# Two down projections computed by seven block products in place of eight

## What is computed

```
# first block
up = conv(h @ w_up) ; val, gate = split(up)
x = x + g2 * ((silu(gate) * val) @ w_down)       # (1024, 2816) @ (2816, 1024)
# second block
a, g = split(h @ ffn_up) ; a = dwconv3x3(a) + b
x = x + gate * ((gelu(a) * g) @ ffn_down)         # the same sizes
```

## Time and profile before

| what | value |
|---|---|
| median of three runs | 2507.37 us |
| the profiled execution | 2507.51 us |
| its span, first to last instruction | 2505.7 us |
| first down projection, first matmul to first of the short units | 904.93 to 1138.49 us |
| short units behind it | 1138.49 to 1183.55 us |
| second down projection to the end of its last unit | 2249.02 to 2487.53 us |
| rows behind it, to the end | 2487.53 to 2505.7 us |

### The profile page before, as it was taken

One profiled execution on the slowest core, in us unless ns is written; L12 is line 12 of the kernel. 1 busy time (PEld: TensorE's weight loads), 2 busy tenths in 40 slices (PEclk: granted clock), 3 DMA queues, 4 the chain that ended last, 5 costly groups with the idle time before them and its releaser, 6 DMA issues. The chain is left out here.

```text
span 2505.7 us, 38163 instructions
## 1 busy us (share of the span) xinstructions
PE 2390.1 (95%) x16353; PEld 1291.5 (52%) x16353; DVE 1634.7 (65%) x2158; ACT 1019.3 (41%) x1219; POOL 561.4 (22%) x296
## 2 busy tenths in 40 slices
PE   7989889999999999999999999988989999999997
PEld 3447664444444444444767776774434444444443
DVE  6788847565545554555477878786878877773343
ACT  5117417345454531323354545442344444441221
POOL 0010000057777711000000000000036766630000
PEclk9999999999999999999999999999999999999998
DMA  9117674121212144443200000003112121225342
GB/s 338 34 53 237 195 229 160 62 73 52 67 51 68 51 148 122 110 109 127 64 26 18 26 26 23 21 26 126 51 51 67 51 68 51 68 64 176 94 114 90
DMA packets 307687, 224.62 MB, mean 90 GB/s; under 512 B 11424, under 2 KB 298302, under 8 KB 306367
## 3 DMA queue, kind: packets, MB, share of 16 engines
q1 hardware_dynamic: 306646, 221.86, 29.3%
q10 hardware_dynamic: 873, 0.32, 0.1%
HBM read 199.61 MB, written 22.03 MB: 88 GB/s over the span
## 5 line engine op out<-in xcount | busy, mean ns | idle before, releaser
L200 PE MATMUL ps<-hT,arena 128*128 128x512 bf16 (+1 forms) x2592 | 552.4, 374 | 15.8 <-DVE arena L2185 5.9
L2118 PE MATMUL ps<-hT,arena 128*128 128x512 bf16 x2280 | 498.9, 379 | 0.3 <-DVE ps L2269 0.3
L1923 PE MATMUL ps<-arena 128*128 128x512 bf16 x2106 | 459.0, 380 | 2.5 <-DVE arena L1907 2.5
L200 PEld LDWEIGHTS ps<-hT,arena 128*128 128x128 bf16 x2592 | 252.7, 98 | 313.3 <-issue 20.3
L2118 PEld LDWEIGHTS ps<-hT,arena 128*128 128x128 bf16 x2280 | 223.0, 98 | 269.8 <-issue 1.3
L1923 PEld LDWEIGHTS ps<-arena 128*128 128x128 bf16 x2106 | 206.3, 98 | 251.8 <-DVE arena L1907 3.8
L2194 POOL TENSOR_TENSOR arena<-arena 128x2048 f32<-128x2048 f32 x2 | 12.6, 6282 | 1138.7 <-DVE arena L696 1138.7
L2407 DVE SCALAR_TENSOR_TENSOR xT<-ps,vec,xT 128x945 f32<-128x945 f32 (+2 forms) x176 | 215.1, 1222 | 31.9 <-ACT xT L2390 26.4
L1907 DVE TENSOR_TENSOR arena<-hT,arena 128x2816 bf16<-128x2816 f32 x30 | 92.8, 3093 | 181.8 <-ACT arena L1902 181.6
L2118 PE MATMUL ps<-xT,arena 128*128 128x512 bf16 x912 | 203.0, 379 | 0.0
L2185 POOL TENSOR_TENSOR arena<-arena 128x2048 bf16<-128x2048 f32 x38 | 156.4, 4115 | 100.6 <-ACT arena L2177 100.6
(11 more groups left out here) (454 smaller groups left out, 3291.8 us busy)
## 6 DMA issues: line engine op xcount, KB each, us to landing
xT<-ada_w_dram SPq DMA_DIRECT2D x24, 1024.0 KB, 5.9
arena<-w_up_dram SPq DMA_DIRECT2D x44, 512.0 KB, 5.1
arena<-ffn_up_dram SPq DMA_DIRECT2D x44, 512.0 KB, 5.2
hT<-w_down_dram SPq DMA_DIRECT2D x30, 704.0 KB, 7.6
hT<-ffn_down_dram SPq DMA_DIRECT2D x30, 704.0 KB, 7.0
arena<-w_in_dram SPq DMA_DIRECT2D x33, 512.0 KB, 4.1
xT<-w_mod_dram SPq DMA_DIRECT2D x16, 1024.0 KB, 6.2
arena<-w_mod_dram SPq DMA_DIRECT2D x8, 1024.0 KB, 19.4
```

What stands on the lines that cost most here:

```text
L200: last = pe.matmul(out, lhs(a, kt), rhs(b, kt, i), start=start and kt == 0 and (a, b) == (0, 0), stop=stop and kt == n_k - 1 and (a, b) == ...
L1923: last = pe.matmul(self.bank(u), self.part(u, a, kt), self.g[:, b, kt, cols], start=kt == 0 and (a, b) == (0, 0), stop=kt == FT - 1 and (a ...
L2118: last = pe.matmul(out, self.stationary(u, block, a, kt), moving(b, kt), start=start and kt == 0 and (a, b) == (0, 0), stop=kt == 3 and (a ...
```

## The change

The contraction (22 row tiles) and the output tiles and tokens are cut in two each, which makes a 2 x 2 by 2 x 2 product of blocks. Seven products replace eight (Winograd's form). DownProducts runs them as 28 jobs (product, n) of 11 x 3 matmuls each, in the order of JOBS. Products 5, 6, 3 and 7 take sums of weight blocks (S1, S2, S4, S3) which POOL adds, 1408 columns at a time, from loaded raw blocks, 16 sums in all. Products 5, 3, 6, 7 and 4 take combinations of g: T1 = x - B11 (POOL, row by row, in the up projection, 22 instructions of 512 columns), T2 (POOL, one instruction of 11 x 512 columns, in place, once the parts of T1 are written), T3 (third_combination, 44 chained additions of 256 columns on DVE at loop steps 9 to 14) and T4 (22 additions of 512 columns on POOL). Their high parts are one ACT instruction and their low parts one DVE instruction of 5632 columns each (operand_hi, operand_lo). All 28 low parts of weights are DVE's (POOL_FROM is 28), 1408 columns each. A product's bank is added to up to three tiles of x, 44 updates. Three banks go on accumulating into a second product (CHAINED), after their updates were read. Raw weights come in 35 DMAs of 704 KB instead of 32. The residual is loaded in three DMAs, two of them ahead of the first job. The first half of m_norm is finished behind the last job, c_norm stands in the last six; the turns of the second half of the tokens in the second block stand behind the last job, with a full sum for each row.

```diff
--- before.py
+++ after.py
...
-class DownByHalves:
...
+            row = u - HALF_K
+            if row >= 0:
+                pool.wait_ge(self.done, row + 1)
+                pool.wait_ge(self.combined, 4 + 2 * row)
+                for part in range(2):
+                    value = self.g_first[:, row, :].rearrange("p (h n) -> p h n", h=2)
+                    if part:
+                        pool.wait_ge(self.combined, 4 + 2 * row + 1)
+                    pool.tensor_tensor(value, value, self.b11[:, row, :, part, :], ALU.subtract).then_inc(self.combined, 1)
...
-        c = self.conv_of(u, 0)
-        dve.tensor_tensor(c, c, self.conv_of(u, 1), ALU.mult).then_inc(self.multiplied, 1)
+        c, gate = self.conv_of(u, 0), self.conv_of(u, 1)
+        dve.tensor_tensor(self.second_half(u), self.second_half(u), gate[:, HALF:T], ALU.mult)
+        dve.tensor_tensor(self.g_first[:, u, :], c[:, 0:HALF], gate[:, 0:HALF], ALU.mult).then_inc(self.multiplied, 1)
...
+class DownProducts:
...
+    JOBS = [(1, 0), (1, 1), (1, 2), (1, 3), (2, 0), (2, 1), (2, 2), (5, 0), (2, 3), (6, 0), (5, 1), (3, 0), (6, 1), (5, 2),
+            (3, 1), (6, 2), (5, 3), (3, 2), (6, 3), (7, 0), (3, 3), (7, 1), (7, 2), (7, 3), (4, 0), (4, 1), (4, 2), (4, 3)]
+    TARGETS = {1: (12, 21, 22), 2: (11,), 5: (12, 22), 6: (21, 22), 3: (12,), 7: (22,), 4: (21,)}
+    CHAINED = {2: 1, 3: 6, 4: 7}
...
+    SUMS = [("S1", 0), ("S2", 0), ("S1", 1), ("S4", 0), ("S2", 1), ("S1", 2), ("S4", 1), ("S2", 2), ("S1", 3), ("S4", 2),
+            ("S2", 3), ("S3", 0), ("S4", 3), ("S3", 1), ("S3", 2), ("S3", 3)]
+    SUM_OF = {5: "S1", 6: "S2", 3: "S4", 7: "S3"}
+    FOURTHS_BEHIND = {("S4", 0): 2, ("S2", 1): 3, ("S2", 2): 3, ("S4", 2): 3}
+    POOL_FROM = 28
+    T1_DONE = 4 + 2 * HALF_K
...
+        sp.wait_ge(f.a_lo, FT)
+        bring(sp, "F", 1, 1, 0, (1, 0))
+        sp.wait_ge(f.s_lo, FT - f.PLAIN)
+        bring(sp, "R3", 1, 1, 1, (1, 1))
+        sp.wait_ge(f.multiplied_out, f.product_count(FT - 1, 6))
+        self.residual(sp, slice(0, 4))
+        sp.wait_ge(f.done, FT - 1)
+        self.residual(sp, slice(4, 6))
+        sp.wait_ge(f.made, f.made_count(FT - 1))
+        bring(sp, "R0", 1, 1, 2, (1, 2))
+        bring(sp, "R1", 1, 1, 3, (1, 3))
+        split(1, 0)
+        bring(sp, "R2", 1, 2, 0, (2, 0))
+        split(1, 1)
+        bring(sp, "R3", 1, 2, 1, (2, 1))
+        sp.wait_ge(f.done, FT)
+        self.residual(sp, slice(6, KD))
+        split(1, 2)
+        bring(sp, "R0", 2, 1, 0, ("A21", 0))
+        split(1, 3)
+        bring(sp, "R1", 2, 2, 0, ("A22", 0))
+        split(2, 0)
+        bring(sp, "R2", 1, 2, 2, (2, 2))
+        split(2, 1)
+        bring(sp, "R3", 1, 2, 3, (2, 3))
+        split(2, 2)
+        bring(sp, "R2", 1, 1, 0, ("A11", 0))
+        for n in range(4):
+            summed("S1", n)
+            bring(sp, "R0", 2, 1, (n + 1) % 4, ("A21", n + 1))
+            if n == 0:
+                split(2, 3)
+                bring(sp, "R3", 1, 2, 0, ("A12", 0))
+            summed("S2", n)
+            split(5, n)
+            if n < 3:
+                bring(sp, "R1", 2, 2, n + 1, ("A22", n + 1))
+            else:
+                bring(sp, "R1", 1, 1, 0, ("A11", 4))
+            if n >= 1:
+                split(3, n - 1)
+                bring(sp, "R3", 1, 2, n, ("A12", n))
+            if n < 3:
+                summed("S4", n)
+                split(6, n)
+                bring(sp, "R2", 1, 1, n + 1, ("A11", n + 1))
...
+    def pe(self, pe, hook=lambda i, kt: None):
+        f = self.f
+        operand_ready = {5: 5, 3: 6, 6: 7, 7: 8, 4: 9}
+        for i, (product, n) in enumerate(self.JOBS):
+            pe.wait_ge(self.lo, i + 1)
+            if (product, n) == (1, 0):
+                pe.wait_ge(f.done, FT - 1)
+            if (product, n) == (2, 0):
+                pe.wait_ge(f.done, FT)
+            if product in operand_ready and n == 0:
+                pe.wait_ge(f.t_lo, operand_ready[product])
+            if product in self.CHAINED:
+                pe.wait_ge(self.read, self.updates_until(self.job(self.CHAINED[product], n)))
+            elif product == 7:
+                pe.wait_ge(self.read, self.updates_until(self.job(2, n)))
+            elif product in (5, 6) and n >= 2:
+                pe.wait_ge(self.read, self.updates_until(self.job(5 if product == 5 else 3, n - 2)))
+            for kt in range(HALF_K):
+                hook(i, kt)
+                for a, b in PASSES:
+                    last = pe.matmul(self.bank(i), self.w[:, i % 2, a, kt, :], self.moving(product, b, kt),
+                                     start=product not in self.CHAINED and kt == 0 and (a, b) == (0, 0),
+                                     stop=kt == HALF_K - 1 and (a, b) == PASSES[-1], skip_group_check=True)
+            last.then_inc(self.made, 1)
...
+    def split_hi(self, act, i):
+        product, n = self.JOBS[i]
+        if i >= 2:
+            act.wait_ge(self.made, i - 1)
+        else:
+            act.wait_ge(self.f.made, self.f.made_count(FT - 2))
+        if product in self.SUM_OF:
+            act.wait_ge(self.f.summed, self.sum_count(self.SUM_OF[product], n))
+        else:
+            slot, count = self.needed[(product, n)]
+            act.wait_ge(self.loaded[slot], count)
+        act.activation(self.w[:, i % 2, 0], self.raw[self.place(i)], ACT.Copy).then_inc(self.hi, 1)
+    def split_lo(self, eng, i):
+        eng.wait_ge(self.hi, i + 1)
+        eng.tensor_tensor(self.w[:, i % 2, 1], self.raw[self.place(i)], self.w[:, i % 2, 0], ALU.subtract).then_inc(self.lo, 1)
...
+    def operand_lo(self, dve, product):
+        f = self.f
+        dve.wait_ge(f.t_hi, {5: 5, 3: 6, 6: 7, 7: 8, 4: 9}[product])
+        hi, lo = (self.operand[product][:, :, s, :] for s in range(2))
+        dve.tensor_tensor(lo, self.value(product), hi, ALU.subtract).then_inc(f.t_lo, 1)
+    def third_combination(self, dve, rows):
+        f = self.f
+        dve.wait_ge(f.combined, self.T2_DONE)
+        dve.wait_ge(self.made, self.job(1, 3) + 1)
+        for r in rows:
+            for h in range(2):
+                last = r == HALF_K - 1 and h == 1
+                f.link(dve.tensor_tensor(self.spare_half, self.b11[:, r, h, 0, :], self.b11[:, r, h, 1, :], ALU.add))
+                done = dve.tensor_tensor(self.t3_f32[:, r, h, :], self.x[:, r, h * HALF // 2:(h + 1) * HALF // 2], self.spare_half,
+                                         ALU.subtract)
+                if last:
+                    done.then_inc(f.apart_set, 1)
+                else:
+                    f.link(done)
+    def update(self, dve, i):
+        product, n = self.JOBS[i]
+        dve.wait_ge(self.made, i + 1)
+        if i == 0:
+            dve.wait_ge(self.x_home, 48)
...
+        for target in self.TARGETS[product]:
+            row, column = divmod(target, 10)
+            t = 4 * (row - 1) + n
+            x = self.k.xT[:, t, 0:HALF] if column == 2 else self.k.xT[:, t, HALF:T]
+            if (t, column) in self.updated:
+                dve.wait_ge(self.read, self.updated[(t, column)])
+            self.read_count += 1
+            self.updated[(t, column)] = self.read_count
+            dve.scalar_tensor_tensor(x, self.bank(i), self.gate(t), x, ALU.mult, ALU.add).then_inc(self.read, 1)
...
+    def act(self, act, also=lambda i: None):
+        for i in range(2, len(self.JOBS)):
+            if i + 1 < len(self.JOBS):
+                self.split_hi(act, i + 1)
+            for step, product in ((2, 5), (3, 3), (5, 6), (17, 7), (20, 4)):
+                if i == step:
+                    self.operand_hi(act, product)
+            also(i)
+    def dve(self, dve, also=lambda i: None):
+        self.read_count, self.updated = 0, {}
+        for i in range(2, len(self.JOBS)):
+            if i + 1 < min(self.POOL_FROM, len(self.JOBS)):
+                self.split_lo(dve, i + 1)
+            if i == 2:
+                self.update(dve, 0)
+            self.update(dve, i - 1)
+            for step, product in ((2, 5), (4, 3), (6, 6), (18, 7), (21, 4)):
+                if i == step:
+                    self.operand_lo(dve, product)
+            if 9 <= i < 15:
+                self.third_combination(dve, range(2 * (i - 9), min(2 * (i - 9) + 2, HALF_K)))
+            also(i)
+        self.update(dve, len(self.JOBS) - 1)
+    def pool(self, pool):
+        f = self.f
+        pool.wait_ge(f.t_lo, 5)
+        pool.wait_ge(f.multiplied, FT)
+        pool.tensor_tensor(self.x, self.y, self.x, ALU.subtract).then_inc(f.combined, 1)
+        count, row = self.T2_DONE, 0
...
+            pool.tensor_tensor(self.raw[out], self.raw[a], self.raw[b], op).then_inc(f.summed, 1)
+            for _ in range(self.FOURTHS_BEHIND.get((name, n), 0)):
+                if row == 0:
+                    pool.wait_ge(self.made, self.job(2, 3) + 1)
+                hi, lo = (self.b21[:, row, s, :] for s in range(2))
+                pool.wait_ge(f.combined, count)
```

(89 more changed lines are left out.)

474 lines of the change are left out of this document (214 added, 260 removed).

## The result

The changed kernel takes 2565.8 us (median), the kernel before beside it 2506.6: a ratio of 1.024, 95% interval 1.0214 to 1.0267. It is slower by some 59 us. The profiled execution took 2563.95 us, with a span of 2562.2 us, 56.5 more than before.

The account below looks back on a forecast made before the run. PE was taken to bound the down projections. Terms of +26.1 us (first stretch), +18.8 (behind it), +16.6 (second) and +5.3 (behind it) gave +66.8 on 2507.4: 2574 us, range 2503 to 2602.

Parts of the forecast that it names:

- Removed matmuls: In each down projection, 924 matmuls in place of 1056: 28.5 us off PE, 57.1 us in all; a job 7.13 us.
- Prices: Lengths of DVE, POOL and ACT pieces in a projection, summing to 127, 92 and 63 us, each under PE's 200.
- Exclusion: In the projections, two-SBUF-input DVE instructions and POOL ones exclude each other for their whole length: 186 of 200 us shared.
- Turns: DVE and POOL pieces alternate, delaying low parts and updates; PE waits 41.8 us in the first projection, 39.1 in the second.
- the walk: Reading DVE's and POOL's queues in order, job by job, for PE's waits: 41.8 / 39.1 us in the two projections.
- Clock: PE runs slower behind waits of over 2.25 us, six in each projection: 14 / 12.9 us lost.
- Behind the projections: Behind the first, short units wait 17.1 us for the norm's finish, +18.8 us; behind the second, sums and transposes, +5.3 us.
- Costed at nothing: POOL's 22 added additions in each up projection, 35 loads for 32 and other pieces were claimed to add no time.
- rival of worse turns: In each projection, late loads make three sum cycles pace PE, 5 us more each: +30, about 2605 us; chance 0.12.
- The rival of no exclusion: In the projections, DVE and POOL pieces miss each other; waits of 18 / 16 us remain: about 2506 us; chance 0.12.

Follow-up runs that it names:

- e2: Changed kernel with 43 of the 44 additions of T3 on DVE left out in each projection (T3 not computed): 2540.5 us, ratio 1.0129.
- e5: Changed kernel with T2, T3 and T4 all on DVE, T3 and T4 in three steps each through PSUM, POOL keeping 16 sums: 2514.1 us, ratio 1.0036.

## Why the prediction held

2574 us were predicted and 2565.8 measured, inside the range and by the mechanism forecast. The sum overshoots by 8.6 us (66.8 predicted, 58.2 in the profile): 3.4 in the waits, 4.5 in the clock and the small terms beside it, 0.7 behind the projections. The range of 99 us holds the rival without exclusion too, so that the number fell into it says little; the waits one by one say more. PE's idle time, as predicted and as the gaps of the timeline give it (us):

| ahead of | first, predicted | first, measured | second, predicted | second, measured |
|---|---|---|---|---|
| job 4 | 1.7 | 0.96 | 3.4 | 2.04 |
| job 5 (T2) | 6.4 | 6.12 | 4.8 | 6.11 |
| jobs 6 to 9 | 3.5 | 3.88 | 3.5 | 3.96 |
| jobs 10 to 13 (T3, T4) | 12.3 | 13.56 | 12.3 | 13.14 |
| job 14 | 10.8 | 7.63 | 10.8 | 9.87 |
| jobs 15 to 19 | 3.4 | 3.43 | 3.4 | 2.99 |
| last jobs | 3.7 | 3.21 | 0.9 | 0.55 |
| sum | 41.8 | 38.8 | 39.1 | 38.7 |

- **Removed matmuls.** A job of 33 takes 7.30 us in the timeline with its modelled end, 14.42 for two: 7.12 each, as costed.
- **Prices.** 1408 columns 1.62 us, 5632 columns 6.01, on POOL 3.16 for a sum that nothing disturbs, all worked out from other lengths, came out within 2%, and so did the 0.42 us for 256 columns. T2 has 12 us of its own in its 13.39, as costed.
- **Exclusion.** As predicted, and shown by the fills. The Trainium skill (SBUF — State Buffer, Who interferes with whom) states that it takes reads on POOL and two SBUF inputs on DVE; this case's traces agree: beside fills a low part takes 1624 ns, and the second additions of T, with one input in PSUM, keep their own length beside POOL's sums (1.76 us for 1536 columns, shown at the end; 1757 ns in the kernel with fills).
- **Turns.** That each chained addition pays one POOL instruction, that jobs 11 and 14 wait for an update behind T3, and that job 5 waits for a low part behind T2: all as the walk had it. Job 14 was oversized by 3.2 us in the first projection, job 5 undersized by 1.3 in the second. The 3.4 us given to job 19 were 2.65.
- **Clock.** The granted clock fell behind each long wait, to 0.95 and 0.93 over the stretches. But 33 matmuls behind 6.12, 9.40 and 7.63 us of idle time took 9.34, 8.59 and 9.32 us instead of 7.30: 1.3 to 2.0 us lost, and 2.5 behind the 9.87 us in the second projection. I had taken 3 us from the earlier trace rows, behind a wait of the same size in another stage. In each projection five waits are followed by longer matmuls, and these add up to 8.7 and 9.2 us, where 14 and 12.9 were put into the sum. This is the term that was sized worst. Its count of waits over 2.25 us isn't borne out either: 66 matmuls behind a wait of 2.70 us took 14.42 us, nothing lost, and 33 behind 2.64 us took 8.97. The 12.9 also fits two long and four short waits, not the split that is written beside it, and no row gives the 1.2 us taken off the first stretch. What is left of the stretches beside matmuls and waits is 10.1 and 4.2 us, predicted 12.8 and 6.0. With the waits that makes +20.4 and +14.4 where 26.1 and 16.6 were predicted.
- **Behind the projections.** 17.04 us of waiting against 17.1, +18.9 on the stretch against +18.8; behind the second +4.5 against 5.3. That the whole finish stands in the way is shown by the kernel that lets PE begin inside it.
- **Costed at nothing.** The up projections and the rest are together some 2 us shorter in the profile, not longer: POOL's 22 added additions in each are hidden there. Loads of weights land in a median of 5.7 and 6.5 us, not 7.6, less than the rival of worse turns took. Sums do wait for loads (42.7 us of POOL's idle time ahead of nine of them in the first projection are ended by one), but no row of the table has the 5 us more a cycle that the rival asked for:

```profile
hT<-w_down_dram SPq DMA_DIRECT2D x18, 704.0 KB, 5.7
hT<-ffn_down_dram SPq DMA_DIRECT2D x18, 704.0 KB, 6.5
```

- **The rival of no exclusion** was put at 2506 us; made real, it is 2490. Its waits were taken as 18 and 16 us, and are 10.2 and 9.5; the longest left in the first projection, in the timeline of PE, is 6.09 us ahead of job 19, which waits for product 7's operand, by the same chain as in e2 (a sum behind a load of 4.91 us, a low part, the operand's low part until 1049.83):

```profile
1049.93 9.61 PE L2499 MATMUL ps<-arena 128*128 128x512 bf16 x33 [6.09 <-issue]
```

With that, the change's value without exclusion is a gain of up to 0.75% (the fills are a little short), where the prediction had called it level.

What stays open: whether another order of the context's and the first half's normalisation would remove more of the junction than 5 us (DVE has 47.5 us of work in the 64 us behind the last job, 31.0 of 45.1 before), and whether the 16 sums could be kept away from DVE's two-input work in time. Neither was tried. Open too is what in e5 won how much, and what sets the time there.

## What to carry to other kernels

Before work is moved to the engine that looks idle, count the two-input instructions of DVE and the reading ones of POOL in the same stretch as one queue: here, by the prices of the prediction, 94 and 92 us of some 200, 186 together, and with POOL's part as fills a loss of 2.4% became a gain of 0.75%. A chain of short DVE instructions pays one POOL instruction for each of its own: 44 additions lasted 45 us instead of 19 in the first projection. With fewer and wider ones, half of them with one input in PSUM, and POOL left with the sums alone, 51 of the 59 us came back. And where an algorithm with fewer products delivers all of its results at the end, price what used to run beside it: here 19 us, two thirds of the saving of one projection.

## What the hardware showed that was not expected

- A DVE addition with one input in PSUM isn't touched by POOL's sums. From the timelines of the kernel with T on DVE in the second projection alone: the sum and the addition run their own length side by side (1757 ns beside fills), and the low part behind it, with two SBUF inputs, waits for the end of the same sum:

```profile
2381.19 3.17 POOL L2656 TENSOR_TENSOR masks<-masks,hT 128x1408 f32<-128x1408 f32 x1 [1.70 <-DMA masks<-ffn_down_dram]
...
2381.22 1.76 DVE L2571 TENSOR_TENSOR arena<-ps,arena 128x1536 f32<-128x1536 f32 x1
2383.01 2.83 DVE L2521 TENSOR_TENSOR arena<-hT,arena 128x1408 bf16<-128x1408 f32 x1
```

- Writing to PSUM instead gives no such freedom: L2570, with two SBUF inputs and its output in PSUM, took 4278 ns, a mean of two that were both issued beside a sum, and 2287 beside fills.
- A DVE busy for 79% of a stretch (179.1 of 226.4 us) doesn't hide what holds it up: with 22 to 23 us less on DVE, the sums being fills, the stretches were 15 to 18 us shorter.
